# Second head's softmax scaling of the wide row tiles moved from GpSimd to ScalarE, at the head of ScalarE's next step

## The reference

```python
p_c = masked_softmax(s_c, cmp_end[None, :] <= t[:, None])     # compressed keys (31)
...
p_s = masked_softmax(s_s, m_s...)                             # selected blocks of 64 keys
...
p_w = masked_softmax(s_w, m_w)                                # sliding window of 512 keys
...
out = gb[..., 0:1] * o_cmp + gb[..., 1:2] * o_sel + gb[..., 2:3] * o_win
```

## Time and profile before

| what | value |
| --- | --- |
| median of three launches | 733.11 us (732.45 to 733.17) |
| the profiled launch, device time | 732.52 us |
| its span in the trace | 730.8 us |
| TensorE busy | 719.0 us, 98% |
| VectorE / ScalarE / GpSimd busy | 511.4 / 331.2 / 150.8 us |
| TensorE's granted clock, mean | 0.996 of full |

### The profile page before, as it was taken

The page is one execution under the profiler, slowest core; times in us unless marked ns, Lnnn a source line. Parts: engine busy times, 40 slices in busy tenths (PEclk is TensorE's granted clock), DMA queues, the critical chain, the costliest instruction groups (busy, mean ns, idle before and its releaser), DMA issues.

```text
span 730.8 us, 11800 instructions
## 1 busy us (share of the span) xinstructions
PE 719.0 (98%) x4347; PEld 638.7 (87%) x4347; DVE 511.4 (70%) x913; ACT 331.2 (45%) x538; POOL 150.8 (21%) x164
## 2 busy tenths in 40 slices
PE   8999999999999999999999999999999999999995
PEld 7889888888888987888899899999999998888884
DVE  3424288797778784765798589999898885223576
ACT  3413377567767776432425154444444443313500
POOL 2608081512334431000000212222222210000000
PEclk9999999999999999999999999999999999999998
DMA  8524315203011204634541132333233334232202
GB/s 254 172 90 128 104 62 162 66 1 98 19 58 59 58 1 115 231 115 155 194 113 58 57 106 72 111 115 115 72 100 115 115 112 153 81 115 92 80 30 86
DMA packets 57459, 73.82 MB, mean 101 GB/s; under 512 B 3888, under 2 KB 44368, under 8 KB 57296
## 3 DMA queue, kind: packets, MB, share of 16 engines
q1 hardware_dynamic: 57280, 72.32, 30.9%
q0 software_dynamic: 144, 1.05, 0.7%
HBM read 70.21 MB, written 2.10 MB: 99 GB/s over the span
## 4 chain that ended last, share of the span: by engine, by line
PE 92%; DVE 4%; ACT 2%; issue 1%; DMA 1%; SPq 0%; DVEq 0%; ACTq 0%
PE ps L1628 83%; PE ps L1640 4%; PE ps L1636 2%; PE ps L1637 2%; ACT prob L874 1%; DVE prob L1287 1%; DVE ptl L1068 1%; DMA arena<-in_x 1%; DVE wl L1068 0%; DVE prob L1241 0%; ACT wh L683 0%; PE ps L1793 0%; PE ps L1794 0%; DVE rinv L1238 0%; DVE rinv L1237 0%
## 5 line engine op out<-in xcount | busy, mean ns | idle before, releaser
L1628 PE MATMUL ps<-wh,xh 128*128 128x512 f32 (+1 forms) x376 | 145.0, 386 | 0.1
L1628 PE MATMUL ps<-wh,xl 128*128 128x512 f32 (+1 forms) x376 | 143.5, 382 | 0.0
L1628 PE MATMUL ps<-wl,xh 128*128 128x512 f32 (+1 forms) x376 | 143.3, 381 | 0.0
L1628 PE MATMUL ps<-xh,wh 128*128 128x256 f32 (+1 forms) x416 | 135.3, 325 | 0.0
L1628 PE MATMUL ps<-xh,wl 128*128 128x256 f32 (+1 forms) x416 | 131.8, 317 | 0.0
L1628 PE MATMUL ps<-xl,wh 128*128 128x256 f32 (+1 forms) x416 | 131.6, 316 | 0.0
L1058 DVE TENSOR_TENSOR wl<-stage,wh 128x2048 fp32r<-128x2048 f32 (+1 forms) x28 | 63.8, 2277 | 92.2 <-ACT wh L689 64.2
L1628 PE MATMUL ps<-ath,wl 128*128 128x256 f32 (+1 forms) x280 | 86.1, 307 | 0.0
L1628 PE MATMUL ps<-atl,wh 128*128 128x256 f32 (+1 forms) x280 | 86.1, 307 | 0.0
L1628 PE MATMUL ps<-ath,wh 128*128 128x256 f32 (+1 forms) x280 | 86.1, 307 | 0.0
L1628 PEld LDWEIGHTS ps<-xh,wl 128*128 128x128 f32 x416 | 79.3, 191 | 5.5
(11 more groups left out here) (285 smaller groups left out, 1349.7 us busy)
## 6 DMA issues: line engine op xcount, KB each, us to landing
stage<-in_w_in SPq DMA_DIRECT2D x28, 512.0 KB, 4.6
stage<-in_w_ffn_gate SPq DMA_DIRECT2D x22, 512.0 KB, 4.8
stage<-in_w_ffn_up SPq DMA_DIRECT2D x22, 512.0 KB, 4.5
stage<-in_w_ffn_down SPq DMA_DIRECT2D x22, 512.0 KB, 3.6
stage<-in_w_out SPq DMA_DIRECT2D x8, 512.0 KB, 4.6
arena<-in_x SPq DMA_DIRECT2D x8, 256.0 KB, 5.9
stage<-in_w_in SPq DMA_DIRECT2D x8, 256.0 KB, 6.2
stage<-in_w_branch_nsa SPq DMA_DIRECT2D x4, 512.0 KB, 6.9
```

The source lines that it names most:

```text
L1628: return pe.matmul(out, (sh, sh, sl)[i], (mh, ml, mh)[i], start=start and i == 0, stop=stop and i == 2)
```

## The change

For tiles with `STEPS[..][0] >= 2`, that is 384 and 512 keys, the second head's scaling leaves GpSimd and becomes a ScalarE multiplication at the very start of ScalarE's pass `i`. It is the same multiplication in place, signalled by the same semaphore. GpSimd keeps the tiles of 128 and 256 keys. There are 16 instructions of this kind, 8 for each width.

```diff
@@ GpSimd
             for i in range(N_STEPS + 3):
-                if i - 1 in SOFT:
+                if i - 1 in SOFT and STEPS[i - 1][0] < 2:
                     a = SOFT[i - 1]
                     n = P * (STEPS[i - 1][0] + 1)
                     pool.wait_ge(rinv_ok, a + 1)
@@ ScalarE
             act.wait_ge(mix_done, 4)
             for i in range(N_STEPS + 3):
+                if i - 1 in SOFT and STEPS[i - 1][0] >= 2:
+                    a = SOFT[i - 1]
+                    p = prob[:, a % 2, 1, 0:P * (STEPS[i - 1][0] + 1)]
+                    act.wait_ge(rinv_ok, a + 1)
+                    act.mul(p, p, rinv[:, a % 2, 1:2]).then_inc(p_ok[1], 1)
                 if 2 <= i < N_STEPS + 2:
                     a = i - 2
                     n = 2 * P * (STEPS[a][0] + 1)
```

## The result

| | before | after |
| --- | --- | --- |
| median | 732.92 us (4 runs, 732.45 to 733.17) | 737.73 us (4 runs, 737.54 to 739.12) |
| ratio to before, 95% interval | | 1.0075 (1.0063 to 1.0087) |
| span of the profiled launch | 730.8 us | 735.8 us |

The kernel became slower by 4.8 us in the medians and by 5.0 us in the spans of the profiled launches. The forecast was 738.3 us (+5.8 on the profiled launch of before), in a range from 735.4 to 741.2.

What follows compares the result with a forecast made beforehand. TensorE was taken as the bound, fed by a ScalarE-VectorE loop almost as long. Delays of `ptl` from br 1's multiplication, less slack and idle time, summed over eight triples to +5.8 us on 732.5: 738.3 us, range 735.4 to 741.2.

Steps and rivals of the forecast that it cites:

- The sum: TensorE's stalls over the eight wide attention triples, adding +5.8 us to the profiled launch of 732.5 us.
- the table: Eight wide triples, tracking VectorE's and TensorE's lateness from delay, slack and idle time; ends at 5.78 us.
- TensorE is the bound, and what it waits is paid: Whole kernel: TensorE busy 719.0 of 730.8 us, so whatever makes it wait is paid in full.
- The multiplication of br 0: On ScalarE between the exponentials, hidden by VectorE's row maximum: costs nothing; without that cover 0.6 us each.
- Its price on ScalarE: Time br 1's added multiplication holds ScalarE: 0.62 us at 512 keys, 0.51 at 384, taken from the exponential.
- `ptl` later by 0.90 us: VectorE's `ptl` after br 1's reciprocal at 512 keys: start moves from t + 0.80 to t + 1.70.
- the added hold by `oth`: VectorE's `otop` waits for `oth`, passing delay on: next row maximum 0.9 us later, 0.75 in triple two.
- The table's rule: Per triple, stall is C + delay - T - slack; next C is C + delay less VectorE's idle time, at least T.
- Two sums of the range: Low end 735.4: half the delay, about 3 us; high end 741.2: 8.7 more, from 6.8 and two delays of 0.9.
- worse backlog: Rival: late merge-gate copies or weight quarters stall TensorE's fill, 3.6 us on top, 741.9; chance 0.1.
- GpSimd's port: Faster rival's second way: GpSimd's scalings hold VectorE up through shared memory access; both ways together chance 0.04.
- The 0.6 us for GpSimd: TensorE's wait in triple eight for GpSimd's scaled head: not subtracted, as a later product waits for `ptl` anyway.

Runs made afterwards that it cites:

- e2: Changed kernel with ScalarE scaling the second head only for br 1, GpSimd keeping br 0: 738.41 us, 732.60 before beside it; ratio 1.0076.
- e1: Changed kernel with ScalarE scaling the second head only for br 0, GpSimd keeping br 1: 732.14 us, 732.60 before beside it; ratio 0.9995.
- e3: Changed kernel with br 1's multiplication moved behind the `pth` copies and output rows (`obot`, `oth`): 732.40 us, 732.60 before beside it; ratio 0.9996.
- e9: Kernel before, with ScalarE instead of VectorE scaling br 0's first head for 384 and 512 keys: 731.87 us, 732.62 before beside it; ratio 0.9990.
- e11: Kernel before, with ScalarE instead of VectorE scaling br 0's first head for all tiles: 730.26 us, 732.62 before beside it; ratio 0.9969.
- e10: Kernel before, with ScalarE scaling both heads of br 0 for 384 and 512 keys: 732.81 us, 732.62 before beside it; ratio 1.0001.
- e7: Kernel before, with ScalarE only waiting for br 1's factor ahead of `pth` in wide tiles, no multiplication: 733.72 us, 732.42 before; ratio 1.0020.
- e6: Changed kernel with the change kept for the 384-key tile alone: 736.74 us, 732.42 before beside it; ratio 1.0061.

## Why the prediction was right, and where it was off

**The size.** The sum was +5.8 us, the stage time says 5.5, the spans 5.0 and the medians 4.8. Only the first difference is one of the table. The next is the 0.53 us by which the changed kernel's launch was ahead at the first load, before any wide triple, and the medians are of four launches each; e2, with the same loss in the stage, has 5.8 us in its medians. So how close 738.3 came to 737.73 is partly luck.

**TensorE is the bound, and what it waits is paid.** Right in the main: +4.7 us in the matmuls' waits for `ptl`, less 0.6 for GpSimd, in a stage that is 5.5 us longer. From the first load to just behind the last (205.35 to 281.00 before, 204.82 to 286.00 after) the matmuls' idle time rose from 1.2 to 5.6 us, and the busy time of the same 453 matmuls from 74.5 to 75.6. That 1.1 us is not explained; the ends of matmuls are modelled in the trace.

**The multiplication of br 0 costs nothing.** Right, by e1.

**Its price on ScalarE.** 0.725 and 0.618 us measured; 0.72 and 0.61 us, those of the exponentials, were taken. The estimate by the rule of the Trainium skill ("ScalarE: Activation LUTs", "What ACT_TABLE_LOAD costs") gave 0.706 and 0.599: the trace agrees within 0.02 us, and the plain copy would have been 0.1 us too low.

**`ptl` later by 0.90 us.** Measured 0.82 in triple three (1.62 - 0.80). The multiplication began at t + 0.40 and not t + 0.45, and `ptl` 0.60 us after `pth` and not 0.63. Over the eight triples the delay was 0.83, 0.61, 0.82, 0.96, 0.79, 0.92, 0.79 and 0.78 us; `ptl` began 1.51 to 1.76 us after the reciprocal, a wider spread than the 1.6 to 1.7 expected.

**The table.** T is TensorE's lateness at the first weight load of each product, C VectorE's at the reciprocal of br 1, both after taking off the 0.53 us by which this launch was ahead at the first load:

| triple | 1 | 2 | 3 | 4 | 5 | 6 | 7 | 8 |
| --- | --- | --- | --- | --- | --- | --- | --- | --- |
| C forecast | 0 | 0.65 | 1.40 | 1.64 | 2.54 | 3.20 | 4.06 | 4.92 |
| C measured | 0 | 0.61 | 1.17 | 1.29 | 2.26 | 2.77 | 3.80 | 4.72 |
| T forecast | 0.45 | 1.25 | 1.54 | 2.44 | 3.20 | 4.06 | 4.71 | 5.78 |
| T measured | 0.34 | 1.15 | 1.20 | 2.08 | 2.84 | 3.69 | 4.33 | 5.51 |

The measured T is 0.3 to 0.4 us lower from triple three on. That gap opens in one place: triple three's stall was 0.05 us (1.20 - 1.15) and not 0.29. The mis-sized term is mainly what triple two passes on. The table has VectorE's next row maximum 0.75 us later, but C rose by only 0.56 (1.17 - 0.61). `ptl` was 0.61 us late there, as forecast, but the added hold by `oth` did not come: `oth` ended at 225.01, and `otop` began at 225.04, when the second `ptl` was ending at 225.06. The delays above matter less, since they are lower by up to 0.08 us in six triples and higher by 0.06 in triples four and six. The table's rule with the measured delays, and with nothing added for `oth` in triple two, ends at 5.4 us, against 5.5 measured: the rule is right, and the terms were a little large.

**Two sums of the range.** By the same rule half of each delay gives 2.5 us, not about 3, so the low end should have been 735.0; and 6.8 plus two further delays of 0.9 is 8.6 and not 8.7. Neither changes what the measurement decides.

**The waits of the fill (worse backlog).** Did not come: the merge-gate copies and weight quarters are later, and no row of the fill's matmuls waits in the changed kernel.

**GpSimd's port.** Not shown to matter: e3 takes all 16 wide scalings off GpSimd and gains 0.2 us in the medians, inside its interval.

**The 0.6 us for GpSimd are not to be gained.** Right: e1 and e3 took that wait away and the medians did not move beyond their intervals. Their traces do have TensorE 0.4 us earlier at triple five, and no more than that at triple eight (0.39 and 0.28). So the wait of triple eight gave nothing, and a small gain may lie ahead of it; which wait that was is not shown.

What stays open: by their stage times e9 should be 1.3 us and e11 0.9 + 1.3 = 2.2 us faster than before; the medians say 0.75 and 2.4. e11 agrees. For e9 the trace shows where the rest went in its profiled launch: behind the last load 450.52 us are left, in place of 449.92, since TensorE waits once more in the FFN stage, for low parts of weights from VectorE:

```profile
587.27 0.39 PE L1655 MATMUL ps<-ath,wh 128*128 128x256 f32 x1 [0.23 <-DVE wl L1093]
```

e10's launch lost as much there (450.57), e11's did not (449.79). Taking off 0.6 us brings e9 to 0.7 and e10 to +0.2, as in their medians. What made `wl` late in these two was not followed up, nor is it known whether all their launches had it.

## What to carry to other kernels

An engine with idle time is not free at every place of its queue. Before an instruction is moved to another engine, ask what stands behind it there and does not need its result: here eight multiplications ahead of the wrong copies cost 5.5 us, and the same eight behind those copies and the output rows, some 1.3 us later, nothing. A wait that ends just after the next instruction would have started costs time even with no work in it (e7, 1.3 us). And the relief belongs where two engines' loops meet: one scaling in each triple taken off VectorE, into ScalarE's wait for VectorE, gave 2.4 us (e11), where the same idle time of the wide tiles given to GpSimd's work gave nothing beyond the noise (e1).

## What the runs showed of the hardware that was not expected

A wait of 2.0 us on TensorE can be followed by a spell at the lower clock: in e6 the granted clock was 0.52 from 282 to 284 us and 0.62 from 284 to 286, which cost 1.0 us (4.18 - 3.20). It does not always come. The changed kernel's profiled launch had the same wait and a granted clock of 1.00 from 280 to 290 us. Of its four launches three had a mean clock of 0.997 to 0.998 and took 737.54 to 737.83 us, and one had 0.994 and took 739.12. Of e6's five, three had 0.994 (736.74 to 737.53 us) and two 0.997 and 0.998 (736.29 and 736.22). e2, whose stall there is split in 0.65 and 1.11 us, had no launch below 0.996 in five. So a stall of this length seems to carry a second price, of about one microsecond, in some launches. Only e6's profiled launch shows it; for the other launches it is inferred from their mean clock, and what decides whether it comes is not shown.
